# Value projection with 512 moving columns from two neighbouring weight slots in a two-layer hybrid trunk

## What is computed

```python
def hybrid_mixer(xn, w_in, ...):
    proj = xn @ w_in
    q, k, v, u_ssm, h_conv, b_gate, c_gate, gate_logits = jnp.split(proj, IN_SPLITS, axis=-1)
    heads = (bsz, l, SB_HEADS, SB_HEAD_DIM)
    y_a = stick_breaking_attention(q.reshape(heads), k.reshape(heads), v.reshape(heads)) @ w_br_a
    y_b = s5_ssm(u_ssm, ...) @ w_br_b
    y_c = short_conv(h_conv, b_gate, c_gate, conv_w) @ w_br_c
    ...
    return merged @ w_out
```

## Time and profile before

| | us |
|---|---|
| median of 3 runs | 1607.51 |
| lowest, highest run | 1607.09, 1607.96 |
| span of the profiled execution | 1607.5 |
| PE busy in it | 1577.3 (98%) |
| PEld busy | 948.6 (59%) |
| DVE busy | 563.7 (35%) |
| ACT busy | 354.0 (22%) |
| POOL busy | 259.5 (16%) |

### The profile page before, as it was taken

How to read it: one execution, slowest core, us unless ns; L and a number is a source line. 1 busy time by engine, 2 the same in 40 slices (tenths; PEclk the granted TensorE clock), 3 DMA queues, 4 the chain that set the end, 5 groups by cost and what they waited for, 6 DMA issues and landing times.

```text
span 1607.5 us, 30983 instructions
## 1 busy us (share of the span) xinstructions
PE 1577.3 (98%) x14113; PEld 948.6 (59%) x14113; DVE 563.7 (35%) x792; ACT 354.0 (22%) x436; POOL 259.5 (16%) x313
## 2 busy tenths in 40 slices
PE   7999999999999999998999999999999999999997
PEld 6988999999999978973333333333333333333332
DVE  5887577655555576560201101110111011101111
ACT  5452354444444552420000000000000000000001
POOL 3437279100000174003000000000000000000060
PEclk9999999999999999999999999999999999999999
DMA  9622489655555401778999999999999999999991
GB/s 275 224 93 79 126 267 392 198 187 182 183 185 182 155 25 58 272 273 338 389 412 420 418 413 414 418 417 409 416 419 416 415 414 417 418 408 420 418 415 79
DMA packets 151940, 484.58 MB, mean 301 GB/s; under 512 B 10720, under 2 KB 92640, under 8 KB 137472
## 3 DMA queue, kind: packets, MB, share of 16 engines
q1 hardware_dynamic: 145232, 467.30, 75.2%
q10 hardware_dynamic: 4816, 10.04, 1.7%
q0 software_dynamic: 1760, 5.24, 0.9%
HBM read 467.22 MB, written 15.34 MB: 300 GB/s over the span
## 4 chain that ended last, share of the span: by engine, by line
PE 68%; DVE 1%; ACT 1%; issue 1%; DVEq 0%; ACTq 0%
PE work L1070 18%; PE acc L1087 18%; PE acc L1070 12%; PE work L720 11%; PE ssm_y L1070 6%; PE work L841 1%; PE ssm_y L848 0%; PE acc L720 0%; PE acc L811 0%; PE work L985 0%; PE work L747 0%; PE acc L803 0%; DVE parts L1432 0%; ACT arena L1395 0%; PE acc L824 0%
## 5 line engine op out<-in xcount | busy, mean ns | idle before, releaser
L720 PE MATMUL work<-xs,parts 128*128 128x256 f32 x3600 | 454.9, 287 | 8.6 <-DVE parts L1432 4.8
L720 PEld LDWEIGHTS work<-xs,parts 128*128 128x128 f32 x3600 | 441.9, 193 | 19.4 <-issue 15.8
L1070 PE MATMUL work<-ring,arena 128*32 128x448 f32 x3072 | 318.4, 539 | 2.5 <-issue 2.2
L1087 PE MATMUL acc<-ring,arena 128*32 128x512 f32 x2688 | 291.0, 592 | 0.0
L1432 DVE TENSOR_TENSOR parts<-ring,parts 128x2048 fp32r<-128x2048 f32 x94 | 220.3, 2348 | 123.0 <-ACT parts L1166 122.9
L1815 DVE TENSOR_TENSOR arena<-arena,work 128x448 f32<-128x448 f32 x48 | 26.9, 616 | 613.2 <-ACT arena L1357 613.2
L1070 PE MATMUL acc<-ring,arena 128*32 128x448 f32 x2048 | 221.6, 541 | 3.3 <-issue 2.5
L1070 PEld LDWEIGHTS work<-ring,arena 128*32 128x32 f32 x3072 | 102.7, 110 | 193.3 <-issue 193.2
L1087 PEld LDWEIGHTS acc<-ring,arena 128*32 128x32 f32 x2688 | 87.4, 110 | 199.5 <-issue 199.5
L1166 ACT ACTIVATE parts<-ring 128x2048 fp32r<-128x2048 f32 x94 | 178.8, 1907 | 89.4 <-PE work L720 62.8
L1357 ACT ACTIVATE arena<-acc 128x448 f32<-128x448 f32 x32 | 15.7, 541 | 676.0 <-PE work L1070 676.0
(11 more groups left out here) (315 smaller groups left out, 1023.1 us busy)
## 6 DMA issues: line engine op xcount, KB each, us to landing
ring<-in_moe_w_gate SPq DMA_DIRECT2D x128, 896.0 KB, 9.1
ring<-in_moe_w_up SPq DMA_DIRECT2D x128, 896.0 KB, 10.0
ring<-in_moe_w_down SPq DMA_DIRECT2D x112, 1024.0 KB, 9.3
ring<-in_w_in SPq DMA_DIRECT2D x44, 1024.0 KB, 6.4
ring<-in_dense_w_gate SPq DMA_DIRECT2D x14, 1024.0 KB, 5.5
ring<-in_dense_w_up SPq DMA_DIRECT2D x14, 1024.0 KB, 5.6
ring<-in_dense_w_down SPq DMA_DIRECT2D x14, 1024.0 KB, 4.9
routed<-arena ACTq DMA_DIRECT2D x1, 9216.0 KB, 31.7
```

The lines of the kernel that those rows point to most:

```text
L720: last = nc.tensor.matmul(out_ap, a, b, start=start and n == 0, stop=stop and n == len(pairs) - 1, skip_group_check=shared)
L1070: last = nc.tensor.matmul(banks[g][GRP * q:GRP * q + GRP, 0:CHUNK], x, w[:, q * CHUNK:q * CHUNK + CHUNK], start=k == 0, stop=k == KT - 1, ...
L1087: last = nc.tensor.matmul(acc[GRP * q:GRP * q + GRP, b, :], eh[:, which, 2 * u + kk, g * GRP:g * GRP + GRP], w[:, kk, half * OUT_COLS:half ...
```

## The change

For v, the roles of the two numbers are swapped: step v0 now makes token tile 0 with all 512 value columns, step v1 token tile 1. A matmul has the same stationary operand as before, and its moving operand takes 256 columns from each of two neighbouring slots of `parts`. Both steps wait for the rest of both units. Since both steps read both units, `used_up` gives the second step for v0 as well as for v1. DVE's copy goes to one token tile of `v`.

```diff
--- before.py
+++ after.py
@@ -542,7 +542,7 @@
                 return work_done, Group(("dense", n * FT + FT - 1)).done
             if name[:2] in ("gA", "gB", "gC", "wo"):
                 return work_done, Group((l, name[:2], 2 * n + 1)).done
-            return work_done, Group((l, name[0], n)).done
+            return work_done, Group((l, name[0], 1 if name[0] == "v" else n)).done
 
         class Splitter:
 
@@ -785,12 +785,15 @@
                                                   stop=k == KT - 1, shared=True)
                         last.then_inc(work_done, 1)
                     elif kind == "v":
-                        w = weights(l, f"v{t}")
-                        for tt in range(TT):
-                            pairs = []
-                            for k in range(KT):
-                                pairs += three(x_parts, w, x_tile(k, slice(tt * P, tt * P + P)), x_tile(k))
-                            last = accumulate(bank[:, tt * UC:tt * UC + UC], pairs)
+                        s = SPLIT.index((l, "v0"))
+                        assert s % PARTS + 1 < PARTS and SPLIT[s + 1] == (l, "v1")
+                        pe.wait_ge(lo_ready, s + 2)
+                        w = parts[:, s % PARTS:s % PARTS + 2, :, :].rearrange("p s q (k n) -> p s q k n", n=UC)
+                        both = bank.rearrange("p (s n) -> p s n", s=2)
+                        for k in range(KT):
+                            for n, (x, q) in enumerate(((0, 0), (0, 1), (1, 0))):
+                                last = nc.tensor.matmul(both, x_parts[x][:, k, t * P:t * P + P], w[:, :, q, k, :],
+                                                        start=k == 0 and n == 0, stop=k == KT - 1 and n == 2)
                         last.then_inc(work_done, 1)
                     elif kind == "z":
                         pe.wait_ge(q_ready, 2 * l + t + 1)
@@ -1562,8 +1565,7 @@
                             .then_inc(k_ready, 1)
                     elif kind == "v":
                         bank = arrived(Group((l, kind, t)))
-                        nc.vector.tensor_copy(v[:, :, t * UC:t * UC + UC],
-                                              bank[:, :].rearrange("p (t n) -> p t n", n=UC)).then_inc(v_ready, 1)
+                        nc.vector.tensor_copy(v[:, t, :], bank[:, :]).then_inc(v_ready, 1)
                     elif kind == "u":
                         bank = arrived(Group((l, kind, t)))
                         nc.vector.tensor_copy(uT[:, :, :].rearrange("p t n -> p (t n)"), bank[:, :])
```

## The result

| | runs | median us | lowest, highest |
|---|---|---|---|
| before | 20 | 1607.12 | 1606.50, 1608.49 |
| changed | 20 | 1609.52 | 1608.03, 1613.48 |

The ratio of changed to before is 1.0016 with a 95% interval of 1.0010 to 1.0023. The change costs 2.4 us, 0.15%. The forecast was 1606.7 in a range of 1605.4 to 1609.3: the direction was wrong and the time is just above the range. "No change by more than 0.2%" holds by the middle value, but the 20 runs resolve more than that.

What follows compares the result with a forecast made beforehand. PE was taken to bound the kernel, waiting for DVE ahead of layer 0's b0. Layer 0 +0.46 and layer 1 -1.29 gave -0.83 us against 1607.5: forecast 1606.7 us, range 1605.4 to 1609.3.

Steps and rivals of the forecast that it cites:

- DVE's chain of tables: Layer 0, behind h0's rest: DVE works without a gap from 58.65 to 70.59, then b0's rest, for which PE waits.
- The wait for both units: Step v0: PE also needs v1's rest, ready 0.89 us ahead in layer 0 and 1.26 in layer 1; costs nothing.
- h0's split: ACT may overwrite v0's slot only after both v steps; in layer 0 h0's rest and b0 come 0.91 us later.
- 2.20 - s: Layer 0: lateness of h0's rest and b0, s being the value stage's shortening; 0.91 us with s = 1.29.
- the pause: PE's wait ahead of b0 in layer 0: grows from 2.76 to 4.96 us, whatever the matmuls gain.
- I take 215 ns: Value projection, each layer: a pair of load and 512-column matmul takes 215 ns, making the stage 1.29 us shorter.
- The gate passes: Full float32 gate matmuls, taken as nearest row: 212.5 ns per pass, load hidden, so wide pairs get 215 ns.
- The end of 227.5 ns: Value projection: bound with 14.2 ns as a fixed price of every pair; the stage takes 10.92 us, 0.69 shorter.
- rival 1: Value projection: a fixed price per pair stays, 227.5 ns; layer 0 +0.75, layer 1 -0.69, time 1607.6 us; 15%.
- The clock gives part of it back: Layer 0, behind b0: full clock returns near 79.03 as before, so 0.45 of the 0.91 us is returned.
- Rival 4: Layer 0: the longer pause lengthens the half-clock stretch from 6.0 to 10.8 us, +2.0 in all, 1609.5 us; 5%.
- The profiled span of 1607.5, which is the median to 0.01: Whole kernel: the base from which the forecast subtracts 0.83 us, taken as the median of three runs.

Runs made afterwards that it cites:

- before, again: The kernel before, unchanged, built and run once more for a second profile: 1594.43 against 1594.93 us, ratio 0.9995.
- layer 1 alone: The kernel before with the whole change made only in layer 1: 1594.14 against 1594.93 us, ratio 0.9996.
- changed, again: The changed kernel, run once more for a second profile and ratio: 1611.76 against 1608.26 us of before, ratio 1.0027.
- wait alone: The kernel before with only v0's slot released after the second v step, matmuls still 256 wide: 1597.97 against 1594.93 us, ratio 1.0021.
- layer 0 alone: The kernel before with the whole change made only in layer 0: 1597.42 against 1594.93 us, ratio 1.0016.
- the filled pair: Before and changed kernels, with 11 and 21 unread PE products in the pause ahead of layer 0's b0: 1594.43 and 1594.58 us.
- before, filled: The kernel before with 11 unread PE products in the pause ahead of layer 0's b0: 1594.43 against 1594.79 us, ratio 0.9999.
- changed, filled: The changed kernel with 21 unread PE products in the pause ahead of layer 0's b0: 1594.58 against 1594.79 us of before, ratio 1.0000.
- table 16 early: The changed kernel with DVE's table of 16 moved ahead of h0's rest: 1608.53 against 1608.26 us of before, then 1593.78 against 1594.79.

## Why the prediction was wrong

**What stood.** PE is the bound and DVE's chain of tables the wait. The wait for both units cost nothing. h0's split moved as worked out: a shift of 2.20 - s with s = 0.61 gives 1.59, and b0 came 1.60 later; the pause grew from 2.76 to 4.97, where 4.96 was worked out. h0, u0 and layer 1 got no new wait.

**"I take 215 ns".** This term was mis-sized: 228 ns. The gate passes are of full float32 and show their pair at its bare streaming time, but the fp32r pairs keep their 14 ns. The end of 227.5 ns, a fixed price per pair, was the right one, and rival 1 with it. The stage gained 0.61 us, not 1.29 (the sum for 227.5 gave 0.69; the last 0.08 is not accounted for). With this alone the sum would have been about +0.1 (0.75 - 0.69), or +0.2 with the measured 0.61.

**"The clock gives part of it back... I take its moment as unchanged".** This step failed. The sum subtracted 0.45 us as a fixed part of every run. The traces show the term as real but not fixed, and the runs show nothing of it:

| trace | pause | PE resumes | full clock | work lost | stretch against 665.45 | sum of terms |
|---|---|---|---|---|---|---|
| before | 2.76 | 73.02 | 79.06 | 3.0 | | |
| before, again | 2.78 | 72.09 | 78.12 | 3.0 | 0.00 | 0.0 |
| layer 1 alone | 2.77 | 72.92 | 78.94 | 3.0 | -0.61 | -0.6 |
| changed | 4.97 | 73.50 | 78.96 | 2.7 | +0.70 | +0.7 |
| changed, again | 4.99 | 73.73 | 76.96 | 1.6 | -0.18 | -0.4 |
| wait alone | 4.99 | 74.32 | 77.18 | 1.4 | +0.85 | +0.6 |
| layer 0 alone | 4.97 | 73.59 | 77.58 | 2.0 | +0.70 | +0.6 |

Work lost is half of the time between the two columns before it. The sum takes +1.6 us for b0 (+2.2 for the wait alone), -0.6 for layer 1 where it is changed, and what is lost less than 3.0. It meets each stretch within 0.3 us, so the traced executions are understood. Behind the start of the stage the full clock returns at 34.2 us in all three traces of the shorter pause, and anywhere from 33.0 to 35.2 in the four of the longer one. Each of these four lost less work to the clock than before's traces, as the prediction had it.

The medians rose all the same, by 2.4 and 3.5 us for the change and 3.0 for the wait alone, where the traces of these kernels say +0.7, -0.2 and +0.9. The traced executions aren't typical: those of the changed kernel (again), the wait alone and layer 0 alone have the lowest times of their sets, 1.9, 1.2 and 0.9 us under the medians, and the two of before lie about 2 and 1.5 us above theirs. So the trace arithmetic accounts for the direction and for +1.0 with a clock that costs both kernels the same. The remaining 1.4 to 2.5 us are in no trace. That they hang on PE's idle time in the pause is what the filled pair points to, within its interval; how they arise stays open.

The mean granted clock of all executions, as time at half clock, fits a clock that costs the longer pause more:

| kernel | mean clock | at half, us |
|---|---|---|
| before (33 runs of a chip of 1595 us) | 0.9962 | 12.2 |
| wait alone | 0.9955 | 14.5 |
| layer 0 alone | 0.9952 | 15.4 |
| layer 1 alone | 0.9964 | 11.6 |
| before, filled | 0.9975 | 8.1 |
| changed, filled | 0.9976 | 7.5 |
| before (23 runs of a chip of 1608 us) | 0.9958 | 13.6 |
| changed, again | 0.9943 | 18.4 |
| table 16 early | 0.9956 | 14.0 |

The last column is 2 x (1 - clock) x span, good to about 1 us since each run's clock is rounded to 0.001. If half of the growth is lost work, as an estimate, the wait alone comes to 2.2 + 2.3 / 2 = 3.3, measured 3.0. Layer 0 alone: 1.6 + 3.2 / 2 = 3.2, measured 2.5. Layer 1 alone: -0.6 - 0.3 = -0.9, measured -0.8. The whole change, on one chip: 1.0 + 4.8 / 2 = 3.4, measured 3.5.

This account fits and is not shown, and four things in the record speak against taking it as proof. The half clock at start-up lasts 3.4 us in the traces of before and 6.8 in those of the changed kernel (again), the wait alone and layer 0 alone, and the value stage starts no later for it; so a difference of 2 to 3 us in the table can be time that costs nothing. Around the pause itself the traces of the longer pause have 6.8, 3.4, 3.4 and 6.8 us at half, and those of before 6.8 each time. Within the 20 runs of the change the time doesn't follow the clock: six with 0.997 average 1609.6 us, and so do six with 0.995. (In the 23 runs of before it does: six with 0.997 or 0.998 average 1606.5, nine with 0.995 average 1608.3.) And filling the kernel before should have given some 2 us and gave 0.4, at the edge of its interval.

**"The profiled span of 1607.5, which is the median to 0.01".** Span and time are not the same thing: a run's time is 1.7 to 1.8 us above its span (2.1 to 3.1 in four of the 11 runs of layer 1 alone). The profile was of an execution slower than the middle. The argument took 3 us of lost work as part of every run of before, so it saw in the longer pause only what was already paid.

**Rival 4** named a half clock that costs more behind a longer pause, as a stretch that grows in proportion to 10.8 us, and gave 1609.5, which is the measured time. That is luck. No trace of the longer pause has more than 6.84 us at half clock, and 1609.5 holds a gain of 1.29 us per layer that isn't there. Rival 1 with a neutral clock, 0.61 gained in each stage and the whole 2.2 of the split kept, gives +1.0, which is what the filled traces show.

**Open.** Two executions each were traced of before and of the change, and one of the others, so how often the clock falls behind a pause of 2.8 and of 5.0 us, and for how long, was not counted. Nothing traced is near the median of the changed kernel. Why the half clock lost behind b0 in before's traces isn't won back in its filled medians is open too.

## What to carry to other kernels

When two steps come to share what each had alone, look at what is released by the first of them: the release moves to the second, and whatever stands in order behind the refill moves with it. Put work that needs nothing ahead of such a refill, as table 16 here, before counting on the gain. Sum against runs, not against one profile. Ask whether a clock dip in the profile is in every execution, and where the traced execution lies among the timed ones.

## What the runs showed of the hardware

- An fp32r pair of load and matmul takes about 14 ns over its streaming time at 256, 384 and 512 moving columns (119 to 121, 176, 227 to 232 ns), in one run of memory or in two of 256. In the same kernel full float32 passes of the same streaming time had 212.5 ns.
- The same kernel with the same pause of 2.96 us fell to the half clock in one execution and not in another, worth 2.6 us. All four traces with a pause of 5.0 us had the fall, with about 3.4 or 6.8 us of half clock, and so had five of the six with a pause of 2.7 to 3.0 us, with 6.8 each.
- Useless products in a pause kept the clock full in each of the three traces where they filled it, at no cost in time that the runs resolve.
